# Prompt attention of a decoder trunk: TensorE makes the scores of step s+2 right behind the turning of step s

## The reference, cut to what matters

```
score = einsum('bqh,bqhs->bqs', wi, relu(logits)) * IDX_SCALE       # indexer, causal
_, sel = lax.top_k(score, 256)
s = einsum('bqhgd,bqkhd->bqhgk', q, k_sel) * HEAD_DIM ** -0.5
p = softmax(where(sel_valid, s, -inf))
o = einsum('bqhgk,bqkhd->bqhgd', p, v_sel)
```

## Time and profile before

| | |
|---|---|
| median of 3 runs | 2544.37 us (2544.36 to 2551.52) |
| the profiled execution | 2544.03 us, its span 2542.3 us |
| granted clock of TensorE, mean | 0.99 |
| PE busy | 2447.4 us, 96% |
| DVE busy | 1821.4 us, 72% |
| ACT busy | 1131.8 us, 45% |
| the prompt attention | about 500 to 681 us of the span |

### The profile page before, as it was taken

One profiled execution on the slowest core, in us unless ns is written; L12 is line 12 of the kernel. 1 busy time (PEld: TensorE's weight loads), 2 busy tenths in 40 slices (PEclk: granted clock), 3 DMA queues, 4 the chain that ended last, 5 costly groups with the idle time before them and its releaser, 6 DMA issues. The chain is left out here.

```text
span 2542.3 us, 49366 instructions
## 1 busy us (share of the span) xinstructions
PE 2447.4 (96%) x18947; PEld 2338.8 (92%) x18978; DVE 1821.4 (72%) x3377; ACT 1131.8 (45%) x1933; POOL 108.5 (4%) x135
## 2 busy tenths in 40 slices
PE   7999988899999999999999999989999999999998
PEld 7899955577899999999999999989999999999998
DVE  6667867787557888886685586764798888667642
ACT  5567577686535343333221453553433333322221
POOL 1310033200000000000000000000000000000000
PEclk9899999999999999999999999999999999999999
DMA  6312399810122343433794423234143434459522
GB/s 212 88 51 78 113 341 376 347 70 1 34 87 69 138 146 137 146 137 124 266 313 137 130 69 115 67 96 166 52 145 138 153 138 154 135 184 341 183 90 84
DMA packets 276591, 371.91 MB, mean 146 GB/s; under 512 B 22152, under 2 KB 215946, under 8 KB 268237
## 3 DMA queue, kind: packets, MB, share of 16 engines
q1 hardware_dynamic: 264573, 294.23, 34.2%
q0 software_dynamic: 11776, 75.50, 7.9%
q10 hardware_dynamic: 80, 0.02, 0.0%
HBM read 271.07 MB, written 98.63 MB: 145 GB/s over the span
## 5 line engine op out<-in xcount | busy, mean ns | idle before, releaser
L1549 PE MATMUL ffn_acc<-trunk_x_ahead,trunk_w_hi 128*128 128x272 f32 x2464 | 466.4, 289 | 2.7 <-PEq L87 2.7
L1549 PE MATMUL ffn_acc<-ffn_x_later,ffn_w_hi_more 128*128 128x272 f32 x2112 | 396.9, 287 | 2.5 <-DVE trunk_xT L1198 1.5
L1549 PEld LDWEIGHTS ffn_acc<-trunk_x_ahead,trunk_w_hi 128*128 128x128 f32 x2464 | 385.2, 188 | 3.3 <-issue 3.3
L1549 PE MATMUL ffn_acc<-trunk_x_ahead,trunk_w_lo 128*128 128x272 f32 x1232 | 352.8, 286 | 0.0
L1549 PEld LDWEIGHTS ffn_acc<-ffn_x_later,ffn_w_hi_more 128*128 128x128 f32 x2112 | 330.8, 188 | 3.1 <-issue 3.1
L1549 PE MATMUL ffn_acc<-ffn_x_later,ffn_w_lo_more 128*128 128x272 f32 x1056 | 303.9, 288 | 0.0
L1549 PEld LDWEIGHTS ffn_acc<-trunk_x_ahead,trunk_w_lo 128*128 128x128 f32 x1232 | 232.5, 189 | 0.0
L1549 PEld LDWEIGHTS ffn_acc<-ffn_x_later,ffn_w_lo_more 128*128 128x128 f32 x1056 | 198.7, 188 | 0.0
L1440 DVE TENSOR_TENSOR trunk_xT<-ffn_acc,trunk_xT 128x544 f32<-128x544 f32 x168 | 121.5, 723 | 102.7 <-PE ffn_acc L1607 101.0
L1607 PE MATMUL ffn_acc<-trunk_x_ahead,trunk_w_hi 128*128 128x272 f32 x896 | 171.3, 289 | 3.8 <-DMA ffn_x_later<-o_kept 1.9
L940 ACT ACTIVATE ffn_w_hi_more<-trunk_w_raw 128x512 fp32r<-128x512 f32 x132 | 83.2, 631 | 159.1 <-PE ffn_acc L1549 154.5
(11 more groups left out here) (521 smaller groups left out, 6000.1 us busy)
## 6 DMA issues: line engine op xcount, KB each, us to landing
o_kept<-trunk_xT SPq DMA_DIRECT2D x96, 544.0 KB, 5.0
trunk_w_raw<-in_ffn_w_gu SPq DMA_DIRECT2D x88, 512.0 KB, 4.0
trunk_x_ahead<-o_kept SPq DMA_DIRECT2D x56, 544.0 KB, 6.7
ffn_x_later<-o_kept SPq DMA_DIRECT2D x56, 544.0 KB, 7.1
x_saved<-trunk_xT SPq DMA_DIRECT2D x24, 544.0 KB, 2.7
trunk_xT<-x_saved SPq DMA_DIRECT2D x24, 544.0 KB, 6.2
o_kept<-trunk_xT SPq DMA_DIRECT2D x32, 272.0 KB, 4.9
trunk_w_raw<-in_sg_w_in SPq DMA_DIRECT2D x16, 512.0 KB, 4.1
```

The costliest lines, as they stand in the source:

```text
L1549: last = nc.tensor.matmul(bank(2 * PAIR[p] + c)[:, 0:QC], w[:, k * P:(k + 1) * P], x(p, k)[:, c * QC:(c + 1) * QC], start=FRESH[p] and k = ...
```

## The change

Within a step of TensorE's program `scores(s + 2)` is issued right behind `turn_probs(s)` instead of at the end of the step. The programs of the other engines, all semaphores and all buffers stay as they are.

```diff
             scores(1)
             for s in range(n_steps):
                 turn_probs(s)
+                if s + 2 < n_steps:
+                    scores(s + 2)
                 if s:
                     values(s - 1)
                 if s >= 2:
                     turn_out(s - 2)
-                if s + 2 < n_steps:
-                    scores(s + 2)
             values(n_steps - 1)
```

## The result

The kernel with the change takes 2552.71 us (median of 15 runs), the one before 2546.05 us (15 runs, those shown ahead of the prediction among them). The medians differ by 6.7 us. The ratio on record is 1.0027, with a 95% interval of 1.0019 to 1.0036: 6.9 us more, 4.8 to 9.2.

What follows compares the result with a forecast made beforehand. TensorE was taken as the bound, fully busy at i = 6 and 7. Terms -0.6 + 1.25 + 2.0 + 3.35 + 1.35 = +7.35 us on 2544.03 give 2551.4, the median 0.34 higher, 2551.7; range 2547.6 to 2554.0.

Steps and rivals of the forecast that it cites:

- Steps 48 to 61: Prompt attention without mask pieces: scale_out late by at most 1.72 us, covered by slack before the turn; cost 0.
- Steps 16 to 25, +1.25: i = 3: late scale_out on ScalarE delays turns in pairs holding a Sign pass; +1.25 us, bounds 0 and 2.2.
- the last term, turn(25): Steps 22 and 23 both hold a Sign pass, so turn(25) takes another 0.47 us.
- Steps 25 to 39, +2.0: i = 1 and 4: scale_out 0.65 us late where ScalarE copies the narrow step; +2.0 us, bounds 0 and 4.6.
- The tie: Four pairs where VectorE copies the narrow step: ScalarE's 0.69 us idle takes up the 0.65; 0.05 allowed for all.
- Mask steps, +3.35: Steps 41 to 48, i = 5: late scale_out on VectorE delays mask pieces and tops; +3.35 us, bounds 1.06 and 6.5.
- turn(63), +1.35: Last turn: step 62 has no scores to cover the late tops behind L3809; +1.35 us, bounds 0 and 1.72.
- First steps, -0.6: Steps 6 to 16: early scores help where their product was last; -0.6 us, between 0 and -0.91.
- the early scores do not win by themselves: Denies rival 1: early maxima fill TensorE's gaps, 0.91 + 2.59 us, down to 2540.9 us; chance 0.08.
- the order doesn't matter: Rival 3: TensorE is the bound and all slack holds; 2543.5 to 2545.5 us, chance 0.07.
- only VectorE's places bite: Rival 2: ScalarE absorbs its delay; +4.1 us, 2548.5 us, chance 0.15.
- Rival 4: The clock falls at new pauses of about 1 us in steps 42 to 48; two falls, 2555 us, chance 0.08.

Runs made afterwards that it cites:

- side_first_act: Changed kernel with the search's Sign pass ahead of scale_out on ScalarE; turn(0) to turn(63) 176.81 us, against 179.49 in the changed kernel.
- early_to_15: Kernel before with scores early in steps 0 to 15 only; turn(0) to turn(63) 172.73 us, against 172.77 before.
- side_first_dve: Changed kernel with VectorE's scale_out moved behind mask pieces and L3809; turn(0) to turn(63) 173.99 us, against 179.49 in the changed kernel.
- side_first_both: Changed kernel with Sign pass, mask pieces and L3809 ahead of scale_out on both engines; ratio to before 0.9993 (0.9980 to 1.0007).
- scores_mid: Kernel before with scores(s+2) moved between values(s-1) and turn_out(s-2); turn(0) to turn(63) 174.82 us, against 172.77 before.
- tops_two_ahead: Changed kernel with tops(s+2) made in step s ahead of VectorE's side work, Sign pass a step later, ahead of scale_out; ratio to before 0.9995.

## Why the prediction was right

The time forecast was 2551.7 us, measured 2552.71. The cost forecast was 7.35 us; the ratio says 6.9, and the trace 6.7. The prediction took 0.3% for about what a measurement can tell; with 15 runs of each the interval is less than 0.1% to either side. The forecast's own mechanism held, place by place:

- **Nothing gained where TensorE is the bound.** Steps 48 to 61: -0.04 us, periods unchanged. The 29.5 us of waits for scores went to 1.7, and here that bought nothing.
- **Steps 16 to 25, +1.25:** measured 1.15. turn(18) to turn(20) takes 4.86 us, the number forecast; the last term, turn(25), was 0.37 for 0.47. `side_first_act` shows the cause.
- **Steps 25 to 39, +2.0:** measured 1.69. The term was mis-sized: 3 x 0.65 were 3 x 0.56 (turn(27) to turn(29) 5.13 against 4.57). I had written that nothing was idle between scale_out and turn(29). In the trace before, the copy of step 28 starts 0.37 us ahead of the exponential; in the one after, 0.26. The exponential had waited for VectorE's maximum for the other 0.11, too short to show as a gap. The tie cost nothing that can be seen: turn(25) to turn(27) is 4.85 in both.
- **Mask steps, +3.35:** measured 3.37, and on the way 1.02, 1.29, 2.18, 2.35 for turns 43, 44, 46, 47, forecast as 1.06, 1.30, 2.24, 2.47.
- **turn(63), +1.35:** measured 1.35.
- **First steps, -0.6:** measured -0.80 in the changed kernel, but -0.03 in `early_to_15`, and -1.67 in `side_first_dve`. The part that is of the order is the same in all of them: -0.74 from turn(6) to turn(16), the steps that the forecast named. Most of it lies from turn(6) to turn(8), 2.42 us against 2.99, the steps in which the first 384-wide scores are made; the 0.91 us of idle time of steps 8 to 15, taken as the bound, hardly changed (0.93). The rest is the clock in the first six steps. That the clock fell for as long in both traces compared here is luck; without its fall the changed kernel's trace would have shown about 5.8 us and not 6.7.

Of the rivals, the early scores do not win by themselves: the rule of the Trainium skill (Perfetto Trace Analysis, Optimization Strategy), to let start sooner what the gaps wait for, pays as it stands from turn(6) to turn(16), 0.74 us. From turn(16) on the trace of the changed kernel disagrees with it (7.5 us longer up to turn(63)), and in steps 24 to 40 it pays only with the queues of the other engines reordered. That the order doesn't matter and that only VectorE's places bite are both excluded by the stretches. The clock did not fall in the new pauses of about 1 us: 1.00 from step 16 on in the changed kernel. Rival 4 priced a fall at 1.7 us; by the traces one costs about 0.9 (last section), and the "long wait" ahead of it was sparse work: TensorE was busy for 1.68 us of the four from 498.81 on, with no pause over 0.71 us. The forecast put slower by over 0.3% at 0.40; the measured 0.27% is on the near side of it.

## What to carry to other kernels

Moving work on the bounding engine moves the deadline and the arrival of everything that it feeds. Before moving it, list what is queued in order behind the first instruction that consumes the delayed result: here it was never scale_out itself that cost, but a scan, a Sign pass and the low part of a finished head, none of which needed its result and all of which stood between it and the next maximum or exponential. Then try the mirror move on the consumer's queue together with the first one; from turn(16) to turn(39) either move alone lost here, 2.8 and 7.0 us, and the pair cost 0.1. A wait that vanishes on an engine that is not the bound is no sign of gain.

## What the runs showed of the hardware

TensorE's clock decides how long the first six steps take. In the trace before it is 0.55 from 502.9 to 506.6. The granted clock behind turn(0), in the changed kernel and in `side_first_both`, whose TensorE program is the same:

```profile
507.15:508.15 1.00, 0.93 (x5) 0.93 (x6) 0.46 (x4) 0.51 (x3) 0.00 (x0) 0.50 1.15 345
508.15:509.15 1.00, 1.00 (x6) 0.82 (x5) 0.39 (x3) 0.56 (x3) 0.00 (x0) 0.50 1.20 301
```

```profile
504.77:505.77 1.00, 0.93 (x8) 0.92 (x8) 0.56 (x4) 0.53 (x4) 0.00 (x0) 1.00 1.14 343
505.77:506.77 1.00, 0.78 (x6) 0.51 (x5) 0.44 (x3) 0.91 (x5) 0.00 (x0) 1.00 1.19 300
```

The first falls to 0.50 (1.2 GHz), the second stays at 1.00 (2.4 GHz). The thirteen traces, cut at turn(6):

| scores in the first 16 steps | fall of the clock | traces | turn(0) to turn(6) | turn(6) to turn(16) |
|---|---|---|---|---|
| old order | about 3.4 us | 5 | 6.81 to 6.91 | 19.18, 19.19 |
| early | none | 4 | 5.88 | 18.43, 18.44 |
| early | about 3.4 us | 2 | 6.74, 6.82 | 18.44 |
| early | 6.8 us | 1 | 7.50 | 18.44 |
| `scores_mid` | about 3.4 us | 1 | 6.75 | 18.96 |

`tops_two_ahead` is one of the four without a fall; its second stretch, 21.00 us, is left out, because its masks delay it. So with early scores a fall of 3.4 us costs 0.9 us and one of 6.8 us 1.6. The five traces of the old order all have a fall and take 6.8 to 6.9 us to turn(6), so up to there the order changes little. From there to turn(16) the early scores gain 0.74 us, whatever the clock did before. Whether the order makes the fall rarer, thirteen traces with one execution each can't settle. In the changed kernel and in `early_to_15` the mean clock up to turn(1) is already 0.59 and 0.74; step 0 is the same in both orders, so those two falls were not brought about by it.
